# Neighbourhood attention by column blocks, and a softmax attention that works on pairs of heads

## The reference, cut to what matters

```python
def neighborhood_attention(q, k, v, kc, vc, rpb):
    ...            # kh = 8 rows, NA_KW = 16 columns, NA_QW = 16, NA_CB = 32
    col_idx = np.clip(np.arange(ncb) * NA_QW - NA_KW // 2, 0, GRID_W - NA_CB)[:, None] + np.arange(NA_CB)[None, :]
    valid = (key_col >= win_start[:, :, None]) & (key_col < win_start[:, :, None] + NA_KW)
    bias = rpb.astype(jnp.float32)[:, dr[:, None, None, :, None], dc[None, :, :, None, :]]
    bias = jnp.where(valid[None, None, :, :, None, :], bias, -jnp.inf)
    ...
    s_loc = jnp.einsum('brnqhd,brnkchd->bhrnqkc', q_blk, k_blk).astype(jnp.float32) * scale + bias
    s_ctx = jnp.einsum('brnqhd,blhd->bhrnql', q_blk, kc).astype(jnp.float32) * scale
    p = jax.nn.softmax(jnp.concatenate([s_loc, s_ctx], axis=-1), axis=-1)
    o = einsum(p_loc, v_blk) + einsum(p_ctx, vc)      # shortened
```

## Time and profile before

| | |
|---|---|
| timed executions, median of 3 | 4304.98 us (4283.55 to 4305.91) |
| profiled execution | 4286.57 us, span 4284.2 us |
| TensorE busy | 3678.6 us, 86% |
| weight loads busy | 3051.4 us, 71% |
| VectorE busy | 2041.0 us, 48% |
| ScalarE busy | 1119.0 us, 26% |
| mean granted TensorE clock | 0.886 |
| HBM | 76 GB/s over the span |

### The profile page before, as it was taken

How to read it: one execution, slowest core, us unless ns; L and a number is a source line. 1 busy time by engine, 2 the same in 40 slices (tenths; PEclk the granted TensorE clock), 3 DMA queues, 4 the chain that set the end, 5 groups by cost and what they waited for, 6 DMA issues and landing times. The chain is left out here.

```text
span 4284.2 us, 50945 instructions
## 1 busy us (share of the span) xinstructions
PE 3678.6 (86%) x20742; PEld 3051.4 (71%) x20742; DVE 2041.0 (48%) x3759; ACT 1119.0 (26%) x1867; POOL 2.7 (0%) x8
## 2 busy tenths in 40 slices
PE   6996998999997987989997984688998883778997
PEld 5986777788886976777875972466887772456886
DVE  3235665433334235664444448754334448664333
ACT  2121443211112131442221321323222321323222
POOL 0000000000000000000000000000000000000000
PEclk9995899999998985999998995779999895679999
DMA  5320000332241200015444320014443320002332
GB/s 188 124 91 5 22 1 30 99 114 85 93 126 62 80 20 25 1 34 169 133 143 125 97 62 0 1 30 137 138 150 125 101 75 0 1 25 74 94 98 74
DMA packets 313562, 326.88 MB, mean 76 GB/s; under 512 B 11211, under 2 KB 229875, under 8 KB 313203
## 3 DMA queue, kind: packets, MB, share of 16 engines
q1 hardware_dynamic: 313330, 323.64, 24.7%
HBM read 321.50 MB, written 2.10 MB: 76 GB/s over the span
## 5 line engine op out<-in xcount | busy, mean ns | idle before, releaser
L1271 DVE TENSOR_TENSOR weights_low<-weights,weights_high 128x1024 fp32r<-128x1024 f32 (+4 forms) x424 | 485.2, 1147 | 1290.7 <-ACT weights_high L933 1288.9
L933 ACT ACTIVATE weights_high<-weights 128x1024 fp32r<-128x1024 f32 (+4 forms) x424 | 422.3, 998 | 1429.6 <-PE bank L493 994.4
L850 PE MATMUL bank<-h_high,weights_high 128*128 128x512 f32 (+1 forms) x1760 | 658.8, 374 | 10.6 <-DVE h_low L1283 9.4
L850 PE MATMUL bank<-h_low,weights_high 128*128 128x512 f32 (+1 forms) x1760 | 649.9, 369 | 0.0
L850 PE MATMUL bank<-h_high,weights_low 128*128 128x512 f32 (+1 forms) x1760 | 648.9, 369 | 0.0
L493 PE MATMUL bank<-weights_high,h_high 128*128 128x426 f32 (+3 forms) x1424 | 519.7, 365 | 19.1 <-DVE h_low L1283 19.1
L493 PE MATMUL bank<-weights_high,h_low 128*128 128x426 f32 (+3 forms) x1424 | 512.7, 360 | 0.0
L493 PE MATMUL bank<-weights_low,h_high 128*128 128x426 f32 (+3 forms) x1424 | 512.5, 360 | 0.0
L850 PEld LDWEIGHTS bank<-h_high,weights_high 128*128 128x128 f32 x1760 | 333.0, 189 | 84.0 <-DVE h_low L1283 17.0
L850 PEld LDWEIGHTS bank<-h_high,weights_low 128*128 128x128 f32 x1760 | 333.0, 189 | 56.0
L850 PEld LDWEIGHTS bank<-h_low,weights_high 128*128 128x128 f32 x1760 | 333.4, 189 | 51.9
(11 more groups left out here) (243 smaller groups left out, 4158.3 us busy)
## 6 DMA issues: line engine op xcount, KB each, us to landing
projected<-in_w_mod SPq DMA_DIRECT2D x80, 1024.0 KB, 5.3
weights<-in_w_gate_up SPq DMA_DIRECT2D x88, 512.0 KB, 4.0
weights<-in_w_down SPq DMA_DIRECT2D x80, 512.0 KB, 3.9
weights<-in_w_in SPq DMA_DIRECT2D x80, 426.0 KB, 3.4
weights<-in_w_gate SPq DMA_DIRECT2D x44, 512.0 KB, 6.7
weights<-in_w_up SPq DMA_DIRECT2D x44, 512.0 KB, 7.7
weights<-in_w_mod SPq DMA_DIRECT2D x32, 512.0 KB, 3.9
weights<-in_w_out SPq DMA_DIRECT2D x32, 512.0 KB, 3.6
```

The costliest lines, as they stand in the source:

```text
L850: mm = pe.matmul(bank[:, 0:cnt], wt[:, k, :], x[:, k, a:a + cnt], start=(k == 0 and q == 0), stop=(k == KD - 1 and q == 2))
L933: act.activation(WH[s_ % 2][:, 0:k * n], slots[j % LAND][:, 0:k * n], ACT.Copy).then_inc(S["w_high"], 1)
L1271: dve.tensor_tensor(WL[s_ % 2][:, 0:k * n], slots[split_of[s_] % LAND][:, 0:k * n], WH[s_ % 2][:, 0:k * n].bitcast(F32), ALU.subtract).the ...
```

## The change

Neighbourhood attention goes by column blocks: the queries of a block of 16 columns form a tile, and see only the 32 columns of keys around it, 256 latent keys in place of 512. The biases for three kinds of block come from the host as six tables of 128x1024 in HBM (`bias_layout`), loaded as weight units, in place of the one-hot matrix. The value columns of N_V are written to HBM and gathered by column block into the place of N_V and of G_K. The scale 0.125 moves into the copies of the turned queries.

One loop, `softmax_attention`, serves neighbourhood and sliding window in one run, and the attention of layers three and four; `mlstm_attention` keeps the old loop for the mLSTM. It works on pairs of heads, one in rows 0 to 63 and one in rows 64 to 127 of the array. Units of one tile of queries form a group of 6 (or 8) heads; its outputs are scaled by one instruction. The weights of the sliding window's queries are ordered so that a pair is one head of each key head; the sink enters as a start value of the maximum and as a term added to the sum.

```diff
+        for n in range(4):
+            v = (0, 1, 1, 2)[n]
+            start = min(max(16 * n - 8, 0), 32)
+            for h in range(NA_H):
...
+                units.append(dict(q=QN[b:b + 64, f, 256 + 128 * n:384 + 128 * n], at=0, keys=[(0, KN[b:b + 64, f, 0:256]), (256, near)],
+                                  n=512, bias=both, table=2 * v + h // 3, sink=None, slot=h, size=6,
+                                  v=[pr(s, N_V + 64 * h, 64) for s in range(CTX_T)]
+                                  + [GATHERED[2 * n + i][:, 64 * h:64 * h + 64] for i in range(2)], y=pr(CTX_T + n, N_Q, 384)))
...
+                def scores(p):
+                    if p >= 1:
+                        pe.wait_ge(S["mix_max"], 2 * p)
+                    a, b = units[2 * p], units[2 * p + 1]
+                    for (at, ka), (_, kb) in zip(a["keys"], b["keys"]):
+                        cnt = ka.size() // ka.shape[0]
+                        pe.matmul(PSA[:, at:at + cnt], a["q"], ka, start=True, stop=True)
+                        mm = pe.matmul(PSA[:, 1024 + at:1024 + at + cnt], b["q"], kb, start=True, stop=True)
+                    mm.then_inc(S["mix_scores"], 1)
...
+                scores(0)
+                for p in range(len(units) // 2):
+                    if p + 1 < len(units) // 2:
+                        scores(p + 1)
+                    turned(2 * p)
+                    turned(2 * p + 1)
+                    values(2 * p)
+                    values(2 * p + 1)
...
-                pe.wait_ge(S["late"], n_late)
-                bank = B.fill(pe, "d")
-                pe.transpose(bank[0:31, 0:90], RPR, ident[0:90, 0:90]).then_inc(S["filled"], 1)
...
-                            mm = pe.matmul(bank[:, 128 * i:128 * i + 128], oh[:, 4 * g + i, :], RPT, start=True, stop=True)
...
+                pe.wait_ge(S["gathered"], 16 * 32)
+                softmax_attention()
...
+                if not second and j == bias_units[0] + LAND:
+                    sp.wait_ge(S["v_saved"], 16)
+                    for i in range(8):
+                        if i == 4:
+                            sp.wait_ge(S["rope"], 1)
+                            sp.dma_start(MASKS, w["masks"]).then_inc(S["masks"], 16)
+                        start = min(max(16 * (i // 2) - 8, 0), 32)
+                        for r in range(4):
+                            row = 64 * (4 * (i % 2) + r) + start
+                            sp.dma_start(GATHERED[i][32 * r:32 * r + 32, :], w["v_na"][row:row + 32, :]).then_inc(S["gathered"], 16)
...
+                exp(0)
+                exp(1)
+                for p in range(len(units) // 2):
+                    u = units[2 * p + 1]
+                    nb = min(u["n"], 512)
+                    if 2 * p + 3 < len(units):
+                        exp(2 * p + 2)
+                    act.wait_ge(S["mix_turn"], 2 * p + 2)
+                    if p:
+                        act.wait_ge(S["mix_values"], 2 * p)
+                    act.activation(PB[1][:, 0:nb], PS[5][:, 0:nb], ACT.Copy).then_inc(S["mix_turned_act"], 1)
+                    if u["n"] > 512:
+                        for e in range(2):
+                            ins = act.activation(PB[e][:, 512:640], PS[6][:, 128 * e:128 * e + 128], ACT.Copy)
+                        ins.then_inc(S["mix_fifth"], 1)
+                    if 2 * p + 3 < len(units):
+                        exp(2 * p + 3)
...
+                    dve.wait_ge(S["mix_scores"], i // 2 + 1)
+                    if i >= 4:
+                        dve.wait_ge(S["mix_turn"], i - 3)
...
+                    dve.tensor_tensor_reduce(to, src, u["bias"], -1.0, first, ALU.add, ALU.min, NMX[:, c:c + 1]).then_inc(S["mix_max"], 1)
...
+                for p in range(len(units) // 2):
+                    if p and first_of_group(units, 2 * p):
+                        output(done)
+                        done = 2 * p
+                    nb = min(units[2 * p]["n"], 512)
+                    if 2 * p + 3 < len(units):
+                        weigh(2 * p + 2)
+                    dve.wait_ge(S["mix_turn"], 2 * p + 1)
+                    if p:
+                        dve.wait_ge(S["mix_values"], 2 * p - 1)
+                    dve.tensor_copy(PB[0][:, 0:nb], PS[4][:, 0:nb]).then_inc(S["mix_turned_dve"], 1)
+                    if 2 * p + 3 < len(units):
+                        weigh(2 * p + 3)
```

More of the change, by code:

```diff
@@ L103, in shape_constants, with bias_layout @@
         c[h, C_SEL + 128 * h:C_SEL + 128 * (h + 1)] = 1.0
[L106 to L114, removed]
+    return c, masks
+def bias_layout(rpb):
+    p, k = np.arange(PT), np.arange(256)
+    r, c, r2, kc = p[:, None] // 16, p[:, None] % 16, k[None, :] // 32, k[None, :] % 32
+    out = np.zeros(rpb.shape[:1] + (6, PT, 1024), rpb.dtype)
+    for v, n in enumerate((0, 1, 3)):
+        col, key = 16 * n + c, min(max(16 * n - 8, 0), 32) + kc
+        start = np.clip(col - 8, 0, 48)
+        inside = (key >= start) & (key < start + 16)
+        row, far = np.broadcast_to(r2 - r + 7, inside.shape), np.clip(key - col + 15, 0, 30)
+        for h in range(6):
+            out[:, 2 * v + h // 3, :, 256 * (h % 3 + 1):256 * (h % 3 + 2)] = np.where(inside, rpb[:, h, row, far], np.float32(NEG))
+    return out
 class Banks:
@@ L275, in layer @@
     else:
-        for j in range(8):
-            unit(w["onehot"][:, UNIT * j:UNIT * (j + 1)], 1, UNIT, split=False)
+        bias_units = [len(weight_units) + j for j in range(6)]
+        for j in range(6):
+            unit(w["bias"][j], 1, UNIT, split=False)
     for j in range(2):
@@ L319, in layer @@
[L319 to L334, removed]
+        QS = SC[:, 4608:6912].rearrange("p (f n) -> p f n", n=TOK)
+        KS = SC[:, 6912:7680]
+        SB = [SC[:, 8448 + 640 * i:8448 + 640 * (i + 1)] for i in range(4)]
@@ L335, in layer @@
+        for t in OUT_T:
+            for i in range(SWA_H):
+                h, b, f = 3 * (i % 2) + i // 2, 64 * (i % 2), i // 2
+                u = dict(q=QS[b:b + 64, f, t * 128:(t + 1) * 128], at=256, keys=[(256, KS[b:b + 64, 0:256])], n=256,
+                         bias=MASKS[:, 0:256], table=None, sink=h, slot=h, size=6,
+                         v=[pr(s, S_V + 64 * (i % 2), 64) for s in range(CTX_T)], y=pr(t, S_Q, 384))
                 if t >= CTX_T:
                     lo, hi = max(t - 1, CTX_T), min(t + 2, NT)
-                    u["kb"] = KS[b:b + 64, kv, lo * 128:hi * 128]
@@ L342, in layer @@
+                units.append(u)
+        n_of_table = [max(i for i, u in enumerate(units) if u["table"] == j) + 1 for j in range(6)]
     else:
```

500 lines of the change are left out of this document (255 added, 245 removed).

## The result

The changed kernel takes 4119.9 us, median of 4 runs (4115.3 to 4126.9), the kernel before 4302.3 in the same comparison: ratio 0.959, 95% interval [0.955, 0.962]. The two profiled executions have spans of 4284.2 and 4125.1 us, 159 apart, where the timed medians are 182 apart: the profiled execution before was 16 us faster than its median, the one after 7 us slower.

What follows compares the result with a forecast made beforehand. TensorE's own work plus two pauses a unit bounds the attention, with bias building ahead of it. Savings of 118 from 4286.6 give 4169, raised by a third of 18 to 4175 us; range 4130 to 4240.

Steps and rivals of the forecast that it cites:

- Layer three 75 against 74, layer four 85 against 85: 0: Attention stages of the last two layers: new loop's time against the old, in us, no gain counted.
- the sum (-118): Whole kernel: layer one -63, layer two -54, layers three and four 0, shorter constants -1.
- five for eight: Scores of a 512-key pair: eight records take five slots of 0.213 us, 1.07; bounds 0.85 and 1.71.
- 63 low us: Layer four's attention: 63 us at half clock before, and 63 assumed after; a low microsecond costs 0.38.
- a third of the 18 us: Profiled execution lay 18 us under the timed median; a third was added, 4169 to 4175.
- Tables out, columns forward: Layers one and two: bias products go, attention starts at 418 instead of 448; 4.4 us of key copies remain, gather hidden.
- Overlap: Scores of two heads in opposite row halves run partly side by side; full halving would take some 10 us off.
- Fused pass, values: 512-key pair: VectorE's bias and minimum in one instruction 0.77 us; 16 value records at 0.111 each.
- The wait for VectorE's copy: 512-key pair of 4.9 us: TensorE waits 0.7 us ahead of the values for VectorE's copy of turned blocks.
- Clock in layers one and two: New loop at half clock for 30 us in layer one and 25 in two, costing 11 and 10 us.
- Granted clock below 0.8: Sign that the forecast is wrong, if seen in the first two layers' stages.
- The rival of a clock low throughout: TensorE idles more, half clock throughout all four attention stages: +57, 4344 us; chance 0.06.

Runs made afterwards that it cites:

- same-half run: Changed kernel with heads of layers three and four paired 0-2, 1-3, 4-6, 5-7, both in one half of the rows: 4196.3 us, ratio 0.973.

## Why the prediction was wrong

*The step that failed: "Layer three 75 against 74, layer four 85 against 85: 0".* It measured -41.7, which is the whole distance from the sum (-118) to the spans' difference (-159). Four errors lie in it.
- The size before was read short: from a window that ended ahead of the last group. From the first weighing to the turned outputs it was 78.2 and 88.5.
- The pairs were taken too long. Slots overlap fully, not five for eight, and the wait for VectorE is shorter. Pairs of 256, 384 and 512 keys took 2.79, 3.54 and 4.46 to 4.57 for 3.1, 4.0 and 4.9. With the text's own conversion (a low microsecond does 0.62 of the work; the pairs above give 0.61) the 33 low and 30 high microseconds of layer three make 50 at full clock, for 61 forecast.
- For the clock of layer four I carried over 63 low us from the earlier trace rows. It was low for 33, as in layer three. Those 30 us at 0.38 are 11, about the difference between -26.0 and -15.7.
- The size before was taken for a constant, and it is a draw: the same code took 68.5 to 101.5 a stage in three traces. The two layers together were 166.7 in the trace that was read, 170.0 and 203.0 in the others, and 125.0 after. A forecast of 0 was wrong against each of them, but -41.7 is no fixed size either. The probable reason why the timed medians are further apart (182) than the spans (159) is this draw; I had gone up by only a third of the 18 us that the profiled execution lay under its median.

*Tables out, columns forward: right.* 30.2 a layer for 30; copies of turned keys 3.8 for 4.4; 16 gathering loads issued in 7.4, out by 411.7 for 410, hidden.

*Overlap: right as a fact, too careful in size.* The Trainium skill, "TensorEngine Tiling (Array Packing)", section Theoretical Speedup, gives up to 2x for a contraction of 64 rows; the trace agrees, with 0.213 for two records of 256 columns. I had put 10 us on that rule and counted slots only. The slots are right, 0.2 a pair (turning starts after 1.07 for 1.27). That same-half stages of layers three and four stayed at half clock, so that the overlap may be worth more than its slots, was not in the working.

*Fused pass, values: right.* 0.69 + 0.08 for 0.77; 16 value records at 0.12 for 0.111.

*The wait for VectorE's copy: right in place, 0.48 for 0.7.* It left the clock alone: full for 89 us with this wait in every pair of 512. What was missing is the other wait, for ScalarE's copies in the pairs of 640. The sum had it as time only (a pair of 7.1; about 6.5 at full clock by the conversion), and 81 of the 134 low microseconds lie from these pairs on.

*Clock in layers one and two: too low a share assumed.* 61 and 73 us at half clock, for 30 and 25. At 0.38 that is +12 and +18. In layer one the shorter pairs outweighed it (-39.6 for -33), in layer two not (-18.8 for -24). These two errors nearly cancel, and in the other traces of the same code the stages sum to 313 to 338 us for 331 here, so that the two stages came out close to the forecast is partly luck. "Granted clock below 0.8" had been named as the sign of a failure: layer two shows 0.76.

*The rival of a clock low throughout* came about in none of the changed kernel's stages, though half clock throughout is real: the same-half run has it in layers three and four, and the old loop in three stages. The Trainium skill, "TensorE: Matmul & The Clock Gate", section The HAM clock gate, says that activity opens the gate. Taken as busy time, the runs contradict it: 96 of 99 us and 81 of 83 us busy stayed at 0.50 and 0.51, while the overlapped pairs of the change, 25.5 of 29 us busy, had 1.00 (2.4 GHz).

What stays open: what moves the clock. In layers three and four it came down in the pairs of 128 keys and rose in larger ones; but pairs of 256 also ran at full clock in layer one (501 to 515), pairs of 512 at half for the first 24 us of layer two, and the old loop did it one way in one execution and another way in the next. The runs show where the clock fell, not why.

## What to carry to other kernels

Two products of half the rows in opposite halves of the array run side by side; here that was 0.85 us in a pair of 512 keys. Waits of TensorE inside a loop can cost more than their length, and the long ones are to be taken out first: in these traces the clock stayed full with 0.48 in a pair and fell in the pairs with 1.1 to 1.6, and a second pair of buffers, which takes both out, was worth 111 us. Before a stage is read as a number, look at the same code in other traces: a stage whose clock moves has no single length. Moving work ahead only moves a wait; look at what it then stands in front of on the other engines, and measure the order again after each change of buffers (the same order gained 42 us with four buffers and cost 81 with two).

## What the runs showed that I had not expected

- Half clock under a full queue: 99 us with TensorE busy for 96, from the first pair to the last, and the same loop with overlapped halves at full clock for its second half.
- Full clock under a queue that has gaps: 1.00 at 25.5 of 29 us busy, and at 77.8 of 88.6.
- The same code of the old loop at half clock for a whole stage of 101.5 us in one place, and for 16 of 68.5 us in another.
- A full-clock TensorE fell back within the small pairs (2509 to 2547) right after 32 large products.
- A switch of order that looks symmetric changed a stage by 32 us in layer one and by 42 in layer two, with the same instructions (executions of one code differ by up to 14 and 12 there).
